# Eight units of an FFN input group in another order

## The chip, the core and the metric

One of the cores of a Trainium2 chip runs the whole program. The metric is the device time of one execution in microseconds (us); a difference is read from the medians of several executions of each kernel.

The core has five engines with queues of their own: TensorE (PE in the profile; PEld is its weight load), VectorE (DVE), ScalarE (ACT), GpSimd (POOL), and SyncE (SP), which here issues nearly all DMAs. Each works its instructions off in order. They meet only at semaphores: an instruction raises one when it is done, another waits until it has reached a value.

## What is computed

A block of 256 tokens by 2048 features passes a half-weighted gated FFN, a token mixer (mLSTM), a second such FFN, and a last norm. The change concerns the two FFNs alone, above all their first product:

```python
D_MODEL = 2048; SEQ = 256; D_FF = 5632
def swiglu_ffn(x, g, w_in, w_out):
    a, b = jnp.split(rmsnorm(x, g) @ w_in, 2, axis=-1)
    return (jax.nn.silu(a) * b) @ w_out
# h = h + 0.5 * swiglu_ffn(h, ffn_norm[i,0], ...)
# h = h + mlstm_mixer(rmsnorm(h), ...)
# h = h + 0.5 * swiglu_ffn(h, ffn_norm[i,1], ...)
# rmsnorm(h)
```

## The kernel before

**Split numbers.** All large products are made of float32 values split into a high and a low part. ACT copies raw weights into `w_hi` (rounded), DVE subtracts and writes `w_lo`, and PE makes three matmuls (high by high, low by high, high by low) for every product of a 128x128 activation block with a 128x512 weight block. The weights are streamed once: SP loads, ACT writes the high part, DVE the low part, PE uses both.

**Groups and units.** The 5632 hidden features of an FFN are made in 11 chunks of 512. The first chunk goes through a plain loop (line 534). The other ten are the *groups*: for each, `a` (left) and `b` (right) come from 16 blocks of 128 input rows. These 16 are taken in pairs, k and k+8, so a group has eight *units*, listed in `UNITS`. A unit that is *plain* makes 8 products (24 matmuls): the left half of its weights goes into the banks p2 and p4 (tokens 0 to 127 and 128 to 255), the right half into p5 and, with differences of activations, into p3. A unit that is *seven* makes a 2x2 block product with seven products (21 matmuls) from sums of activations (`s_hi`, `s_lo`) and mixed weights that DVE makes (`mix_weights`); it adds to p1, p2, p3, p5, p7, p6 and p4 in this order. Only the sevens write p1, p6 and p7. The order before is plain, seven, plain, seven, plain, seven, plain, plain.

**Items and slots.** A plain unit takes one *item* of split weights (two halves), a seven two items (straight weights, then mixed weights), so a group has 11 items. There are three slots for raw weights and three for split ones; ACT may write half of an item only when PE has used that half of the item three back (`pair_used`), and SP may load only when DVE is through with the raw unit three back (`pair_low`).

**Draining a group.** When a group's products are done they are gathered from the banks. ACT copies p1 (`keep_first`, line 1058). DVE then runs, in this order and in its one queue with the `w_lo` work: `drain_products` (p6 and p7 into `sums`; lines 1560, 1562; it waits for the last seven of the group), `drain_left` (p2 and p4 into `tile`; line 1569; it waits for the left half of unit 7), `drain_right` (p5; line 1576) and `drain_last` (p3; line 1583; it waits for all of unit 7). Each raises `drained`. PE may start the left half of the next group's first unit only after `drain_left`, its right half only after `drain_last`. ACT's `silu` and DVE's `gate_hidden` (line 1505) then make the hidden chunk, which PE turns (line 594, four 128x128 transposes each, after units 1 and 2 of the next group) and ACT keeps as `g32` (`keep_hidden`, line 1050).

**From the last group to the second product.** After group 9 the second product of the FFN starts (`ffn_out`; `plain` and `seven` units too, over `g_hi`, `g_lo`). Its first unit writes p2 and p4 again, and so waits for `drain_left` of group 9, as a next group would. DVE's queue at this place is: `w_lo` of units 6 and 7, `drain_products`, `low_hidden(0)` (line 1694), the two `w_lo` halves of the first output unit (line 1702), `low_hidden(1)`, `drain_left`, `drain_right`, `drain_last`. ACT's `high_hidden` (line 1115) writes `g_hi`, whose first two blocks lie over the buffer `mixed`.

Nothing is planned at run time: the order on every engine is the order in which the code is written.

Of the kernel before, what the change touches and what calls it, by code (L numbers as in the profile page):

```python
# [15 lines left out]
GK = 2  # L16
RING = 4
EPS = 1e-6
UNITS = (("plain", 3), ("seven", 0), ("plain", 4), ("seven", 1), ("plain", 5), ("seven", 2),
         ("plain", 6), ("plain", 7))  # L20
SEVENS, PLAINS = 3, 5
FIRST_ITEM = (0, 1, 3, 4, 6, 7, 9, 10)
ITEMS = 11
SLOTS = 3
DRAINS = 5
# [5 lines left out]
def trunk_program(nc, x, ffn_norm, ffn_w_in, ffn_w_out, mix_norm, a_w_in, a_b_if, a_head_norm,  # L31
# [38 lines left out]
    PAIR_HALVES = 2 * ITEMS * GROUPS  # L70
# [31 lines left out]
    def item(group, u):  # L102
        return ITEMS * group + FIRST_ITEM[u]

    def halves(i, n):
        return PAIR_HALVES * i + 2 * n
# [4 lines left out]
    with ExitStack() as ctx:  # L111
# [150 lines left out]
        pair_low = sem("pair_low")  # L262
        pair_used = sem("pair_used")
# [679 lines left out]
        def _(act):  # L943
# [83 lines left out]
            def high_straight(i, group, u):  # L1027

                n, unit = item(group, u), len(UNITS) * group + u
                act.wait_ge(left_landed[unit % SLOTS], landings(i, unit))  # L1030
                act.wait_ge(right_landed[unit % SLOTS], landings(i, unit))
                free(i, n, 1)
                nc.scalar.activation(hi_slots[n % SLOTS][:, 0:3], raw_slots[unit % SLOTS][:, 0:3], ACT.Copy)\  # L1033
                    .then_inc(pair_high, 2)
# [17 lines left out]

            def keep_first(i, group):

                act.wait_ge(pair_used, halves(i, item(group, 5)) + 1)
                if group:
                    act.wait_ge(drained, DRAINS * (GROUPS * i + group - 1) + 3)
                nc.scalar.activation(sums[:, 0, :], p1, ACT.Copy).then_inc(first_kept, 1)
# [11 lines left out]
            def ffn_in(i):  # L1070

                g = G_FFN[i]
                act.wait_ge(rstd_ready, 2 * i + 1)
                split(g + GD, 2, 3)
                silu_first(i)
                split(g + GD, 3, 5)
                high_sides(i)
                split(g + GD, 5, 6)
                high_differences(i)
                split(g + GD, 6, 8)  # L1080
                for group in range(GROUPS):
                    if group == 0:
                        high_plain(i, group, 0, 0)
                        high_plain(i, group, 0, 1)
                    high_straight(i, group, 1)
                    high_mixed(i, group, 1, 0)
                    if group:
                        silu(i, group - 1)
                    high_mixed(i, group, 1, 1)
                    high_plain(i, group, 2, 0)  # L1090
                    high_plain(i, group, 2, 1)
                    high_straight(i, group, 3)
                    keep_hidden(i, group, 0)
                    high_mixed(i, group, 3, 0)
                    high_mixed(i, group, 3, 1)
                    high_plain(i, group, 4, 0)
                    high_plain(i, group, 4, 1)
                    keep_hidden(i, group, 1)
                    high_straight(i, group, 5)
                    high_mixed(i, group, 5, 0)  # L1100
                    high_mixed(i, group, 5, 1)
                    high_plain(i, group, 6, 0)
                    high_plain(i, group, 6, 1)
                    keep_first(i, group)
                    high_plain(i, group, 7, 0)
                    high_plain(i, group, 7, 1)
                    if group < GROUPS - 1:
                        high_plain(i, group + 1, 0, 0)
                        high_plain(i, group + 1, 0, 1)

            def high_hidden(i, b):

                act.wait_ge(hidden_kept, 2 * (NF * i + b) + 2)
                act.wait_ge(pair_used, PAIR_HALVES * (i + 1) - (0 if b > 1 else 4))
                nc.scalar.activation(g_hi[:, 4 * b:4 * b + 4], g32[:, 4 * b:4 * b + 4], ACT.Copy)\
                    .then_inc(hidden_high, 1)

# [301 lines left out]
        def _(dve):  # L1419
# [116 lines left out]
            def mix_weights(i, group, u):  # L1536

                unit, s = len(UNITS) * group + u, SEVENS * (GROUPS * i + group) + UNITS[u][1]
                src = raw_slots[unit % SLOTS]
                if group == 0 and UNITS[u][1] == 0:  # L1540
                    dve.wait_ge(sides_low, 2 * i + 2)
                else:
                    pg, pu = (group, u - 2) if UNITS[u][1] else (group - 1, 5)
                    dve.wait_ge(pair_low, halves(i, item(pg, pu) + 2))
                dve.wait_ge(left_landed[unit % SLOTS], landings(i, unit))
                dve.wait_ge(right_landed[unit % SLOTS], landings(i, unit))
                nc.vector.tensor_tensor(mixed[:, 0:2], src[:, 0:3:2], src[:, 3:4].to_broadcast([P, 2, COLS]),
                                        ALU.subtract).then_inc(mixed_ready, 1)
                dve.wait_ge(mixed_ready, 3 * s + 1)
                nc.vector.tensor_tensor(mixed[:, 2], src[:, 2], mixed[:, 0], ALU.add).then_inc(mixed_ready, 1)  # L1550
                dve.wait_ge(mixed_ready, 3 * s + 2)
                nc.vector.tensor_tensor(mixed[:, 3], src[:, 1], mixed[:, 2], ALU.subtract)\
                    .then_inc(mixed_ready, 1)

            def drain_products(i, group):

                done = DRAINS * (GROUPS * i + group)
                dve.wait_ge(first_kept, GROUPS * i + group + 1)
                dve.wait_ge(pair_used, halves(i, item(group, 5) + 2))
                nc.vector.tensor_tensor(sums[:, 2], p6, sums[:, 0], ALU.add).then_inc(drained, 1)  # L1560
                dve.wait_ge(drained, done + 1)
                nc.vector.tensor_tensor(sums[:, 1], p7, sums[:, 2], ALU.add).then_inc(drained, 1)
# [76 lines left out]
            def ffn_in(i):  # L1639

                g = G_FFN[i]
                split(g + GD, 2, 3)
                sum_sides()
                split(g + GD, 3, 4)
                sum_differences()
                split(g + GD, 4, 5)
                low_sides(i)
                split(g + GD, 5, 6)
                low_differences(i)
                split(g + GD, 6, 8)  # L1650
                for group in range(GROUPS):
                    if group == 0:
                        low_plain(i, group, 0, 0)
                        low_plain(i, group, 0, 1)
                    mix_weights(i, group, 1)
                    low_straight(i, group, 1)
                    if group:
                        drain_left(i, group - 1)
                        low_mixed(i, group, 1, 0)
                        drain_right(i, group - 1)  # L1660
                        drain_last(i, group - 1)
                        low_mixed(i, group, 1, 1)
                        gate_hidden(i, group - 1)
                    else:
                        gate_first(i)
                        low_mixed(i, group, 1, 0)
                        low_mixed(i, group, 1, 1)
                    low_plain(i, group, 2, 0)
                    low_plain(i, group, 2, 1)
                    mix_weights(i, group, 3)  # L1670
                    low_straight(i, group, 3)
                    low_mixed(i, group, 3, 0)
                    low_mixed(i, group, 3, 1)
                    low_plain(i, group, 4, 0)
                    low_plain(i, group, 4, 1)
                    mix_weights(i, group, 5)
                    low_straight(i, group, 5)
                    low_mixed(i, group, 5, 0)
                    low_mixed(i, group, 5, 1)
                    low_plain(i, group, 6, 0)  # L1680
                    low_plain(i, group, 6, 1)
                    low_plain(i, group, 7, 0)
                    low_plain(i, group, 7, 1)
                    if group < GROUPS - 1:
                        low_plain(i, group + 1, 0, 0)
                        drain_products(i, group)
                        low_plain(i, group + 1, 0, 1)
                    else:
                        drain_products(i, group)

            def low_hidden(i, b):

# [446 lines left out]
```

## Time and profile before

| | us |
|---|---|
| Median of 3 executions (lowest, highest) | 1821.99 (1821.84, 1822.6) |
| The profiled execution, its own time | 1822.63 |
| Its span in the trace | 1820.9 |
| PE busy, share of the span | 1802.5, 99% |
| DVE busy | 1455.0, 80% |
| ACT busy | 976.5, 54% |
| Matmuls of lines 599 to 601 (all units, both FFNs) in the chain that ended last | about 70% |

The first number of a row of the timeline is the start in us from the start of the span, the second the time that the row's instructions took together, `x2` how many rows of one kind it merges; what stands in brackets is the idle time of that engine before it and who released it. A matmul's row says 0.39 us, but matmuls overlap: the pace of PE is the distance from one start to the next.

### The profile page before, as it was taken

To read this page: it belongs to the slowest core of one execution; us is meant where nothing else is said; L and a number is where in the kernel's file an instruction comes from. 1 tells how busy PE (TensorE), PEld (TensorE's weight loads), DVE (VectorE), ACT (ScalarE), POOL (GpSimd) and SP (SyncE) were. 2 spreads that over 40 slices of the span, in tenths; PEclk is the share of its full clock that TensorE was granted. 3 is DMA by queue.
4 is the path that set the end of the run, shared out by engine and by line. 5 is a ranking of instruction groups with operands and counts; after the bars stand their busy time and mean duration, and the time that the engine had idled before them with its cause. 6 is when DMAs were issued, how large, how long until landed. Compare 5 with 4: busy or idle time off the path is not lost.

```text
span 1820.9 us, 21509 instructions
## 1 busy us (share of the span) xinstructions
PE 1802.5 (99%) x8107; PEld 1488.4 (82%) x8107; DVE 1455.0 (80%) x1697; ACT 976.5 (54%) x1092; POOL 48.7 (3%) x58
## 2 busy tenths in 40 slices
PE   8999999999999999999999999999999999999998
PEld 6888888888888888888888888888888888888886
DVE  6888888888888886655478757888888888888787
ACT  6555555555555554544445445555555555555453
POOL 0000000000000002000000000000000000000002
PEclk9999999999999999999999999999999999999999
DMA  6666655556666556566645556666666556666564
GB/s 224 219 208 207 206 195 198 185 190 203 205 203 196 187 178 185 154 185 197 196 141 160 163 185 194 210 206 209 204 195 204 185 186 207 199 203 200 185 196 151
DMA packets 180612, 350.71 MB, mean 193 GB/s; under 512 B 10848, under 2 KB 11040, under 8 KB 180256
## 3 DMA queue, kind: packets, MB, share of 16 engines
q1 hardware_dynamic: 179952, 348.17, 59.5%
q0 software_dynamic: 432, 1.18, 0.2%
q8 instruction: 62, 1.02, 0.2%
q14 instruction: 38, 0.31, 0.1%
q10 hardware_dynamic: 128, 0.03, 0.0%
HBM read 347.24 MB, written 2.10 MB: 192 GB/s over the span
## 4 chain that ended last, share of the span: by engine, by line
PE 97%; ACT 1%; DVE 1%; issue 0%; DMA 0%; ACTq 0%; DVEq 0%
PE acc L534 23%; PE acc L599 12%; PE acc L601 12%; PE acc L600 12%; PE aux L599 11%; PE aux L601 11%; PE aux L600 11%; PE aux L594 1%; PE aux L563 1%; PE aux L902 1%; PE aux L890 0%; DMA h<-in_x_dram 0%; ACT u_hi L966 0%; PE aux L852 0%; DVE w_lo L1433 0%
## 5 line engine op out<-in xcount | busy, mean ns | idle before, releaser
L1433 DVE TENSOR_TENSOR w_lo<-raw,w_hi 128x1024 fp32r<-128x1024 f32 x160 | 194.9, 1229 | 107.7 <-ACT w_hi L951 106.2
L951 ACT ACTIVATE w_hi<-raw 128x1024 fp32r<-128x1024 f32 x160 | 168.4, 1059 | 123.6 <-PE acc L534 109.1
L534 PE MATMUL acc<-w_hi,u_hi 128*128 128x512 f32 x512 | 205.6, 401 | 4.2 <-DVE w_lo L1433 4.2
L534 PE MATMUL acc<-w_hi,u_lo 128*128 128x512 f32 x512 | 200.8, 392 | 0.0
L534 PE MATMUL acc<-w_lo,u_hi 128*128 128x512 f32 x512 | 200.3, 391 | 0.0
L1515 DVE TENSOR_TENSOR w_lo<-raw,w_hi 128x1024 fp32r<-128x1024 f32 x112 | 135.2, 1222 | 51.3 <-ACT w_hi L1024 51.3
L1024 ACT ACTIVATE w_hi<-raw 128x1024 fp32r<-128x1024 f32 x112 | 116.4, 1058 | 87.4 <-PE aux L601 46.4
L599 PE MATMUL acc<-w_hi,u_hi 128*128 128x512 f32 x358 | 140.7, 393 | 0.0
L601 PE MATMUL acc<-w_hi,u_lo 128*128 128x512 f32 x358 | 139.6, 390 | 0.0
L600 PE MATMUL acc<-w_lo,u_hi 128*128 128x512 f32 x358 | 139.4, 389 | 0.0
L534 PEld LDWEIGHTS acc<-w_hi,u_hi 128*128 128x128 f32 x512 | 96.7, 189 | 24.7 <-issue 5.0
L534 PEld LDWEIGHTS acc<-w_hi,u_lo 128*128 128x128 f32 x512 | 96.7, 189 | 21.0
L534 PEld LDWEIGHTS acc<-w_lo,u_hi 128*128 128x128 f32 x512 | 96.8, 189 | 19.2
L1702 DVE TENSOR_TENSOR w_lo<-raw,w_hi 128x1024 fp32r<-128x1024 f32 x62 | 75.0, 1233 | 27.6 <-ACT w_hi L1133 26.5
L1532 DVE TENSOR_TENSOR w_lo<-mixed,w_hi 128x1024 fp32r<-128x1024 f32 x72 | 85.7, 1218 | 1.7
L1133 ACT ACTIVATE w_hi<-raw 128x1024 fp32r<-128x1024 f32 x62 | 64.3, 1056 | 42.6 <-PE acc L601 19.8
L599 PE MATMUL acc<-w_hi,g_hi 128*128 128x512 f32 x216 | 84.4, 391 | 0.0
L1042 ACT ACTIVATE w_hi<-mixed 128x1024 fp32r<-128x1024 f32 x72 | 74.5, 1052 | 17.9 <-PE acc L601 17.9
L601 PE MATMUL acc<-w_hi,g_lo 128*128 128x512 f32 x216 | 84.1, 389 | 0.0
L600 PE MATMUL acc<-w_lo,g_hi 128*128 128x512 f32 x216 | 84.1, 389 | 0.0
L1033 ACT ACTIVATE w_hi<-raw 128x1536 fp32r<-128x1536 f32 x28 | 41.8, 1492 | 75.6 <-PE aux L601 66.8
L601 PE MATMUL aux<-w_hi,g_lo 128*128 128x512 f32 x205 | 79.8, 389 | 0.0
(322 smaller groups left out, 4523.6 us busy)
## 6 DMA issues: line engine op xcount, KB each, us to landing
raw<-in_ffn_w_in_dram SPq DMA_DIRECT2D x248, 512.0 KB, 4.5
raw<-in_ffn_w_out_dram SPq DMA_DIRECT2D x124, 512.0 KB, 4.9
raw_more<-in_ffn_w_in_dram SPq DMA_DIRECT2D x104, 512.0 KB, 4.5
raw<-in_a_w_in_dram SPq DMA_DIRECT2D x96, 512.0 KB, 4.2
raw_again<-in_ffn_w_out_dram SPq DMA_DIRECT2D x52, 512.0 KB, 5.4
raw<-in_a_w_out_dram SPq DMA_DIRECT2D x32, 512.0 KB, 4.4
h<-in_x_dram SPq DMA_DIRECT2D x4, 512.0 KB, 8.8
final_gain<-in_final_norm_dram POOLq DMA_DIRECT2D x1, 1024.0 KB, 6.8
```

The lines of the kernel that those rows point to most:

```text
L534: mm = nc.tensor.matmul(acc[:, TT * (c % 2) + t, :], s[:, k, tok], w[:, ring, kk, :], start=(k == 0 and n == 0), stop=(k == GK * granules ...
L599: nc.tensor.matmul(bank, side_hi, wide_hi, start=start, stop=False)
L600: nc.tensor.matmul(bank, side_hi, wide_lo, start=False, stop=False)
L601: return nc.tensor.matmul(bank, side_lo, wide_hi, start=False, stop=stop)
L951: nc.scalar.activation(w_hi[:, n % RING], raw[:, n % RING], ACT.Copy)\
L1024: nc.scalar.activation(hi_slots[n % SLOTS][:, at], raw_slots[unit % SLOTS][:, at], ACT.Copy)\
L1042: nc.scalar.activation(hi_slots[n % SLOTS][:, at], mixed[:, at], ACT.Copy)\
L1133: nc.scalar.activation(out_hi[n % SLOTS][:, at], out_raw[slot][:, at], ACT.Copy)\
L1433: nc.vector.tensor_tensor(w_lo[:, n % RING], raw[:, n % RING], w_hi[:, n % RING].bitcast(F32), ALU.subtract)\
L1515: nc.vector.tensor_tensor(lo_slots[n % SLOTS][:, at], raw_slots[unit % SLOTS][:, at], hi_slots[n % SLOTS][:, at].bitcast(F32), ALU.subtract)\
L1532: nc.vector.tensor_tensor(lo_slots[n % SLOTS][:, at], mixed[:, at], hi_slots[n % SLOTS][:, at].bitcast(F32), ALU.subtract)\
L1702: nc.vector.tensor_tensor(out_lo[n % SLOTS][:, at], out_raw[slot][:, at], out_hi[n % SLOTS][:, at].bitcast(F32), ALU.subtract)\
```

## The change

`UNITS` and the item numbers get another order: plain, plain, seven, plain, seven, plain, seven, plain. A group's last seven is now unit 6 of 7 (before, unit 5 of 7), and its first is unit 2. The bodies of the loops on ACT and DVE are written in the new order; `keep_first` and `drain_products` wait for the last seven at its new place; `drain_left`, `drain_right` and `drain_last` stand among the `w_lo` work of unit 1 of the next group. In `ffn_out` nothing is written anew but the wait of the first two `high_hidden`, which is now for the `w_lo` of the last seven (the last reader of `mixed`).

```diff
-UNITS = (("plain", 3), ("seven", 0), ("plain", 4), ("seven", 1), ("plain", 5), ("seven", 2),
-         ("plain", 6), ("plain", 7))
+UNITS = (("plain", 3), ("plain", 4), ("seven", 0), ("plain", 5), ("seven", 1), ("plain", 6),
+         ("seven", 2), ("plain", 7))
-FIRST_ITEM = (0, 1, 3, 4, 6, 7, 9, 10)
+FIRST_ITEM = (0, 1, 2, 4, 5, 7, 8, 10)
@@ keep_first (ACT)
-                act.wait_ge(pair_used, halves(i, item(group, 5)) + 1)
+                act.wait_ge(pair_used, halves(i, item(group, 6)) + 1)
@@ high_hidden (ACT)
-                act.wait_ge(pair_used, PAIR_HALVES * (i + 1) - (0 if b > 1 else 4))
+                if b > 1:
+                    act.wait_ge(pair_used, PAIR_HALVES * (i + 1))
+                else:
+                    act.wait_ge(pair_low, PAIR_HALVES * (i + 1) - 2)
@@ drain_products (DVE)
-                dve.wait_ge(pair_used, halves(i, item(group, 5) + 2))
+                dve.wait_ge(pair_used, halves(i, item(group, 6) + 2))
@@ ffn_in (DVE)
-                    mix_weights(i, group, 1)
-                    low_straight(i, group, 1)
+                    low_plain(i, group, 1, 0)
                     if group:
                         drain_left(i, group - 1)
-                        low_mixed(i, group, 1, 0)
+                        low_plain(i, group, 1, 1)
                         drain_right(i, group - 1)
                         drain_last(i, group - 1)
-                        low_mixed(i, group, 1, 1)
+                        mix_weights(i, group, 2)
                         gate_hidden(i, group - 1)
...
                     if group < GROUPS - 1:
                         low_plain(i, group + 1, 0, 0)
-                        drain_products(i, group)
                         low_plain(i, group + 1, 0, 1)
-                    else:
-                        drain_products(i, group)
+                    drain_products(i, group)
```

The first place is DVE's queue from one group to the next. `w_lo` rows of 128x1024 are half a plain unit, the 128x1536 row is the straight part of a seven, `mixed` rows are its mixed weights; `sums<-acc,sums` are `drain_products`, `tile<-acc,sums` is `drain_left`, `sums<-aux,sums` of 128x1024 and 128x512 are `drain_right` and `drain_last`. Before:

```order
L1515 TENSOR_TENSOR w_lo<-raw,w_hi 128x1024 [waits pair_high] x3
L1560 TENSOR_TENSOR sums<-acc,sums 128x512 [waits pair_used,first_kept]
L1562 TENSOR_TENSOR sums<-acc,sums 128x512 [waits drained]
L1515 TENSOR_TENSOR w_lo<-raw,w_hi 128x1024 [waits pair_high]
L1547 TENSOR_TENSOR mixed<-raw_more 128x1024 [waits right_landed2,left_landed2,pair_low]
L1550 TENSOR_TENSOR mixed<-raw_more,mixed 128x512 [waits mixed_ready]
L1552 TENSOR_TENSOR mixed<-raw_more,mixed 128x512 [waits mixed_ready]
L1523 TENSOR_TENSOR w_lo_more<-raw_more,w_hi_more 128x1536 [waits pair_high]
L1569 TENSOR_TENSOR tile<-acc,sums 128x1024 [waits drained,hidden_turned,pair_used]
L1532 TENSOR_TENSOR w_lo<-mixed,w_hi 128x1024 [waits pair_high]
L1576 TENSOR_TENSOR sums<-aux,sums 128x1024 [waits drained,right_summed]
L1583 TENSOR_TENSOR sums<-aux,sums 128x512 [waits drained,pair_used]
```

The same place after (line numbers are three higher there):

```order
L1518 TENSOR_TENSOR w_lo<-raw,w_hi 128x1024 [waits pair_high] x4
L1563 TENSOR_TENSOR sums<-acc,sums 128x512 [waits pair_used,first_kept]
L1565 TENSOR_TENSOR sums<-acc,sums 128x512 [waits drained]
L1518 TENSOR_TENSOR w_lo_more<-raw_more,w_hi_more 128x1024 [waits pair_high]
L1572 TENSOR_TENSOR tile<-acc,sums 128x1024 [waits drained,hidden_turned,pair_used]
L1518 TENSOR_TENSOR w_lo_more<-raw_more,w_hi_more 128x1024 [waits pair_high]
L1579 TENSOR_TENSOR sums<-aux,sums 128x1024 [waits drained,right_summed]
L1586 TENSOR_TENSOR sums<-aux,sums 128x512 [waits drained,pair_used]
```

Between `drain_products` and `drain_left` there stood five instructions and there now stands one; the mixing of weights has moved behind `drain_last`.

The second place is DVE's queue at the end of the last group, where the second product of the FFN begins (`g_lo` is `low_hidden`; the `w_lo` row between the two is the first output unit). Before:

```order
L1523 TENSOR_TENSOR w_lo<-raw_more,w_hi 128x1536 [waits pair_high]
L1532 TENSOR_TENSOR w_lo_more<-mixed,w_hi_more 128x1024 [waits pair_high] x2
L1515 TENSOR_TENSOR w_lo<-raw,w_hi 128x1024 [waits pair_high] x4
L1560 TENSOR_TENSOR sums<-acc,sums 128x512 [waits pair_used,first_kept]
L1562 TENSOR_TENSOR sums<-acc,sums 128x512 [waits drained]
L1694 TENSOR_TENSOR g_lo<-g,g_hi 128x1024 [waits hidden_high]
L1702 TENSOR_TENSOR w_lo<-raw,w_hi 128x1024 [waits out_high] x2
L1694 TENSOR_TENSOR g_lo<-g,g_hi 128x1024 [waits hidden_high]
L1569 TENSOR_TENSOR tile<-acc,sums 128x1024 [waits drained,hidden_turned,pair_used]
```

After:

```order
L1526 TENSOR_TENSOR w_lo_more<-raw,w_hi_more 128x1536 [waits pair_high]
L1535 TENSOR_TENSOR w_lo<-mixed,w_hi 128x1024 [waits pair_high] x2
L1518 TENSOR_TENSOR w_lo<-raw,w_hi 128x1024 [waits pair_high] x2
L1563 TENSOR_TENSOR sums<-acc,sums 128x512 [waits pair_used,first_kept]
L1565 TENSOR_TENSOR sums<-acc,sums 128x512 [waits drained]
L1695 TENSOR_TENSOR g_lo<-g,g_hi 128x1024 [waits hidden_high]
L1703 TENSOR_TENSOR w_lo<-raw,w_hi 128x1024 [waits out_high] x2
L1695 TENSOR_TENSOR g_lo<-g,g_hi 128x1024 [waits hidden_high]
L1572 TENSOR_TENSOR tile<-acc,sums 128x1024 [waits drained,hidden_turned,pair_used]
```

The seven now ends one plain unit later: four halves of `w_lo` stood between it and the drain, two stand there now. From `drain_products` on the order is the same.

## Rows read from the trace of the kernel before

**Rows 1.** Waits of PE: what waited for what, total us, times, longest.
```profile
PE acc L534 <- DVE w_lo L1433: 4.2, 4, 2.4
```
**Rows 2.** Timeline of PE, first turn of two groups in succession.
```profile
282.23 0.60 PE L594 MATMUL aux<-ident,tile 128*128 128x128 f32 x4
...
324.68 0.60 PE L594 MATMUL aux<-ident,tile 128*128 128x128 f32 x4
```
**Rows 3.** Timeline of PE, last group: start of unit 7, start of the output.
```profile
478.82 0.39 PE L599 MATMUL acc<-w_hi,u_hi 128*128 128x512 f32 x1
...
484.26 0.39 PE L599 MATMUL acc<-w_hi,g_hi 128*128 128x512 f32 x1
```
**Rows 4.** Timeline of DVE, end of the last group.
```profile
471.76 2.36 DVE L1515 TENSOR_TENSOR w_lo<-raw,w_hi 128x1024 fp32r<-128x1024 f32 x2 [0.56 <-ACT w_hi L1024]
474.04 0.68 DVE L1560 TENSOR_TENSOR sums<-acc,sums 128x512 f32<-128x512 f32 x1
...
475.36 1.22 DVE L1694 TENSOR_TENSOR g_lo<-g,g_hi 128x1024 fp32r<-128x1024 f32 x1
...
481.31 1.22 DVE L1694 TENSOR_TENSOR g_lo<-g,g_hi 128x1024 fp32r<-128x1024 f32 x1
482.45 1.22 DVE L1569 TENSOR_TENSOR tile<-acc,sums 128x1024 f32<-128x1024 f32 x1
```
**Rows 5.** Timeline of PE, a matmul of the mixer that starts as another chunk ends.
```profile
1040.55 0.39 PE L534 MATMUL acc<-w_hi,y_hi 128*128 128x512 f32 x1
```
**Rows 6.** Timeline of DVE, the instruction that the end of that chunk releases.
```profile
1040.74 1.29 DVE L1634 SCALAR_TENSOR_TENSOR tile<-acc,h 128x512 f32<-128x512 f32 x2 [0.34 <-PE acc L534]
```
**Rows 7.** Timeline of DVE, a drain in the second FFN's output.
```profile
1694.71 1.22 DVE L1804 SCALAR_TENSOR_TENSOR tile<-acc,tile 128x1024 f32<-128x1024 f32 x1
```
**Rows 8.** Timeline of PE, which waits for that drain.
```profile
1695.38 0.39 PE L601 MATMUL aux<-w_hi,g_lo 128*128 128x512 f32 x1
1695.98 0.50 PE L599 MATMUL acc<-u_hi,g_hi 128*128 128x512 f32 x1 [0.22 <-DVE tile L1804]
1696.32 0.40 PE L600 MATMUL acc<-u_lo,g_hi 128*128 128x512 f32 x1
```
**Rows 9.** Timeline of ACT, end of the last group.
```profile
470.18 0.60 ACT L1058 ACTIVATE sums<-aux 128x512 f32<-128x512 f32 x1 [0.24 <-PE acc L601]
...
476.36 1.06 ACT L1133 ACTIVATE w_hi<-raw 128x1024 fp32r<-128x1024 f32 x1 [1.66 <-PE acc L601]
```
**Rows 10.** Timeline of PE, second FFN: start of the output.
```profile
1577.68 0.39 PE L599 MATMUL acc<-w_hi,g_hi 128*128 128x512 f32 x1
```
**Rows 11.** Timeline of DVE, second FFN: drain_left of the last group.
```profile
1575.87 1.22 DVE L1569 TENSOR_TENSOR tile<-acc,sums 128x1024 f32<-128x1024 f32 x1
```
**Rows 12.** Timeline of PE, group boundary: right half of unit 7, next group.
```profile
269.31 0.39 PE L599 MATMUL aux<-w_hi,u_hi 128*128 128x512 f32 x1
...
272.03 0.39 PE L599 MATMUL acc<-w_hi,u_hi 128*128 128x512 f32 x1
```
**Rows 13.** Timeline of DVE at that boundary: the drains.
```profile
270.14 1.22 DVE L1569 TENSOR_TENSOR tile<-acc,sums 128x1024 f32<-128x1024 f32 x1
...
272.40 1.22 DVE L1576 TENSOR_TENSOR sums<-aux,sums 128x1024 f32<-128x1024 f32 x1
273.72 0.69 DVE L1583 TENSOR_TENSOR sums<-aux,sums 128x512 f32<-128x512 f32 x1
```
**Rows 14.** The page's DMA issues: count, size, median us from issue to landing.
```profile
raw<-in_ffn_w_in_dram SPq DMA_DIRECT2D x248, 512.0 KB, 4.5
```
**Rows 15.** Timeline of PE, start of the mixer: the longest wait of PE in mid-program.
```profile
739.39 0.39 PE L534 MATMUL acc<-w_hi,u_lo 128*128 128x512 f32 x1
740.69 0.47 PE L534 MATMUL acc<-w_hi,u_hi 128*128 128x512 f32 x1 [0.91 <-DVE w_lo L1433]
```
**Rows 16.** Timeline of PE, two of the twelve matmuls from 9.84 us on.
```profile
14.24 0.63 PE L534 MATMUL acc<-w_lo,u_hi 128*128 128x512 f32 x1
14.67 0.63 PE L534 MATMUL acc<-w_hi,u_lo 128*128 128x512 f32 x1
```

More of the change, by code:

```diff
@@ L1084, in ffn_in @@
                         high_plain(i, group, 0, 1)
-                    high_straight(i, group, 1)
-                    high_mixed(i, group, 1, 0)
+                    high_plain(i, group, 1, 0)
+                    high_plain(i, group, 1, 1)
                     if group:
                         silu(i, group - 1)
[L1089 to L1092, printed above, removed]
+                    high_straight(i, group, 2)
+                    high_mixed(i, group, 2, 0)
+                    high_mixed(i, group, 2, 1)
+                    high_plain(i, group, 3, 0)
+                    high_plain(i, group, 3, 1)
                     keep_hidden(i, group, 0)
[L1094 to L1097, printed above, removed]
+                    high_straight(i, group, 4)
                     keep_hidden(i, group, 1)
[L1099 to L1104, printed above, removed]
+                    high_mixed(i, group, 4, 0)
+                    high_mixed(i, group, 4, 1)
+                    high_plain(i, group, 5, 0)
+                    high_plain(i, group, 5, 1)
+                    high_straight(i, group, 6)
+                    high_mixed(i, group, 6, 0)
+                    high_mixed(i, group, 6, 1)
                     high_plain(i, group, 7, 0)
                     high_plain(i, group, 7, 1)
+                    keep_first(i, group)
                     if group < GROUPS - 1:
@@ L1542, in mix_weights @@
                 else:
-                    pg, pu = (group, u - 2) if UNITS[u][1] else (group - 1, 5)
+                    pg, pu = (group, u - 2) if UNITS[u][1] else (group - 1, 6)
                     dve.wait_ge(pair_low, halves(i, item(pg, pu) + 2))
@@ L1665, in ffn_in @@
                         gate_first(i)
[L1666 to L1681, printed above, removed]
+                        low_plain(i, group, 1, 1)
+                        mix_weights(i, group, 2)
+                    low_straight(i, group, 2)
+                    low_mixed(i, group, 2, 0)
+                    low_mixed(i, group, 2, 1)
+                    low_plain(i, group, 3, 0)
+                    low_plain(i, group, 3, 1)
+                    mix_weights(i, group, 4)
+                    low_straight(i, group, 4)
+                    low_mixed(i, group, 4, 0)
+                    low_mixed(i, group, 4, 1)
+                    low_plain(i, group, 5, 0)
+                    low_plain(i, group, 5, 1)
+                    mix_weights(i, group, 6)
+                    low_straight(i, group, 6)
+                    low_mixed(i, group, 6, 0)
+                    low_mixed(i, group, 6, 1)
                     low_plain(i, group, 7, 0)
```

## The prediction, made before the changed kernel ran

> **What bounds the kernel now.** I read the waits of PE first, then the timeline of PE across several groups, then DVE and ACT at the places where PE depends on them.
>
> PE is the bound without a gap. Its waits on other engines in the whole span, apart from the load of the input, are 4.2 us for `w_lo` in the plain loops [rows 1] and 0.22 us for one drain in an output stage [rows 8]; none lies in the twenty groups. The groups come at a fixed period: the same turn is at 282.23 and at 324.68, so 42.45 us [rows 2], which is 183 matmuls (5 x 24 + 3 x 21) and eight short transposes. A plain unit takes 484.26 - 478.82 = 5.44 us for 24 matmuls [rows 3], 0.2267 us each; a seven, 21 of them, takes 4.76 us. The change leaves every matmul, DMA and split in place. So in the groups it can gain nothing: where PE never waits there is no wait to remove. What can change is that PE meets a wait which was hidden, and the question is how much room each of them has.
>
> Two waits have little room. I call B the moment at which PE is through with unit 7 and wants to start the next stretch.
>
> At a boundary between groups B = 272.03 [rows 12]. `drain_left` ended at 270.14 + 1.22 = 271.36, `drain_last` at 273.72 + 0.69 = 274.41 [rows 13]. PE wants the first at B and the second at B + 2.72 = 274.75 (half a plain unit later): room of 0.67 and 0.34 us.
>
> At the end of the last group B = 484.26 [rows 3]; `drain_left` ended at 482.45 + 1.22 = 483.67 [rows 4]: room of 0.59 us. The second FFN repeats this: 1575.87 + 1.22 = 1577.09 against 1577.68 [rows 10, 11].
>
> **The change at a boundary between groups (18 times).** The last seven now ends at B - 5.44, not at B - 10.88. `drain_products` needs it. How fast DVE answers to PE: a matmul's successor starts at 1040.55, the DVE instruction that this end released at 1040.74 [rows 5, 6], so 0.19 us. ACT answers in 0.26: its row at 476.36 was released by the left half that ended at 484.26 - 5.44 - 2.72 = 476.10 [rows 3, 9].
>
> ACT comes first. `keep_first` needs the first two products of the seven, at B - 10.20 + 1.36 = B - 8.84; it starts at B - 8.58 and takes 0.60 [rows 9]. Then two ACT copies of at most 1.06 each [rows 9] for the next group's unit 0 end by B - 5.9, and DVE's second half of `w_lo` for it by about B - 4.7 (1.22 each [rows 4]). `drain_products` could start at B - 5.44 + 0.19 = B - 5.25 and starts at B - 4.7. It takes 475.36 - 474.04 = 1.32 [rows 4]: B - 3.4. One half `w_lo` follows; back to back such an instruction costs 482.45 - 481.31 = 1.14 [rows 4] (the pair of 2.36 at 471.76 is the same, 1.14 + 1.22): B - 2.26. `drain_left` may start from B - 2.72 + 0.19, so it starts at B - 2.26 and ends at B - 1.04. A second half `w_lo` ends its turn at B + 0.02, `drain_right` passes in 273.72 - 272.40 = 1.32 [rows 13], and `drain_last` ends at B + 1.34 + 0.69 = B + 2.03, wanted at B + 2.72. Room 1.04 and 0.69 us, more than before. Cost: nothing. The mixing for the seven, now behind `drain_last`, is wanted at B + 10.88, and is done by about B + 7.5 (three instructions, `gate_hidden`, the straight part): room of over 3 us. Loads wait for `w_lo` of the unit three back, whose DVE work ends at least 7 us before B for all three first units, against 4.5 us from issue to landing [rows 14]. What hides all this is PE's own work; the cover is 1.04 and 0.69 us, and each 0.1 us by which a drain overran it would cost 18 x 0.1 = 1.8 us.
>
> **The change at the end of the last group (twice).** Here DVE's queue has more between `drain_products` and `drain_left`: `low_hidden(0)`, two halves of the first output unit, `low_hidden(1)`. Before, the first of them started long before PE needed the drain (`drain_products` at B - 10.22 [rows 3, 4]), and DVE idled between them. Now the queue stops at `drain_products` until B - 5.25. DVE is free from B - 7.6: ACT's copy of unit 7's right half is released at B - 10.20 + 0.26, and 1.06 + 1.22 later `w_lo` is through; `keep_first` is done at B - 8.0 as above. So the start is set by PE's seven, and the rest is a sum:
>
> start B - 5.44 + 0.19 = B - 5.25; `drain_products` 1.32; four instructions of 128x1024 back to back at 1.14 = 4.56; `drain_left` 1.22. End: B + 1.85.
>
> Does ACT hold it up? Its copies for the first output unit need the two halves of the seven's second item, used at B - 6.80 and B - 5.44, so they end at latest at B - 5.5 and B - 3.5, `high_hidden(1)` between them at B - 4.5, each before DVE comes to it (B - 2.8 to B - 0.5). The new condition on `high_hidden` (`w_lo` of the last seven, about B - 11.4) is met long before. No.
>
> PE restarts after the drain. Where it waits for one before, the drain ends at 1694.71 + 1.22 = 1695.93 and PE starts at 1695.98 [rows 7, 8]: 0.05; the next matmul comes 0.34 later and not 0.23 [rows 8], 0.11 more. So one transition costs 1.85 + 0.05 + 0.11 = 2.01 us, two cost 4.0 us. Bounds for one: none at all if the drain came in its 0.59 us of room as before; 2.7 if each of the five back-to-back instructions before the drain took the 0.1 more that single ones show to PE's restart elsewhere (740.69 comes 1.30 after 739.39, and a copy before it may be late by as much [rows 15]). I take the sum, since all its terms are rows of the same instructions in the same place.
>
> What is late next: `drain_last` then ends at B + 1.85 + 0.10 + 1.32 + 0.69 = about B + 4.0, wanted at B + 1.90 + 2.72 = B + 4.6; `w_lo` of the second output unit by B + 6.6, its left half by B + 5.5, wanted from B + 7.4. These hold, with 0.6 us as the least.
>
> Sum against the profiled execution: 1822.63 + 4.0 = 1826.6; its own time is 0.64 above the median of the runs, so the median goes from 1821.99 to 1826.0. A measurement of this kernel tells about 0.2% from no change, 3.6 us; the forecast is just beyond it.
>
> **Rivals.**
>
> 1. The delay is taken back later. In the first FFN's wake PE waits in the mixer's start (1.30 us from 739.39 to 740.69, of which 0.23 is its pace [rows 15]), and it waits 0.6 - 0.23 = 0.37 before 1695.98 [rows 8]; all `w_lo` waits together are 4.2 us, the longest 2.4 of them at the start [rows 1]. If these hung on DMA or on work that doesn't move with PE, up to 4.2 - 2.4 = 1.8 and 0.4 us would be absorbed: 4.0 - 2.2 = 1.8 us, 1823.8, not slower by what can be told. For it: those are waits on DVE and ACT, not on PE. Against it: their chains begin with results that PE has just made. It decides if PE's waits after the stall shrink.
>
> 2. The groups stall too. The boundary keeps 0.69 us of room by a sum of many terms. If DVE's queue there is a microsecond later than I make it, `drain_last` costs some 0.3 us each time: 18 x 0.3 + 4.0 = 9.4, 1831.4. For it: before, the room was as small, so nothing is loose. Against: the sum gives more room than before with the same instructions.
>
> 3. The clock falls in the new gap. Before, twelve matmuls after the first wait came 14.67 - 14.24 = 0.43 us apart [rows 16], 512 columns at 1.2 GHz, against 0.227 at 2.4 GHz later. Twelve such after each gap of 1.9 us cost 2 x 12 x 0.20 = 4.8 more: 1830.8. Against: after the 0.91 us idle before 740.69 the engine went on with 0.47 us for a matmul, not 0.63 [rows 15]. No row has a gap of 1.9 us at full clock. The Trainium skill (TensorE: Matmul & The Clock Gate, section HAM oscillation) warns of just this, waits between bursts of matmuls that bring the clock down each time; no run here shows how long a gap must be.
>
> 4. The order does nothing: no wait of PE appears, 1822.0. It would need the last seven's products to be free earlier than B - 5.44; the order of DVE's rows speaks against it.
>
> **How the numbers follow.** Forecast 0.70, of which 0.12 for a sum that comes out under 3.6 us (it is 4.0, with some 0.2 for the answer times and as much for the medians). Rival 1: 0.11. Rival 2: 0.07. Rival 3: 0.05. Rival 4 and what I overlook, 0.07: half of it no change, half divided between faster (0.03) and slower. So slower 0.58 + 0.07 + 0.05 + 0.01 = 0.71, same 0.12 + 0.11 + 0.03 = 0.26, faster 0.03. The range of the forecast alone is 1825.2 to 1827.4 (2.7 a time at the top). To hold eight in ten it reaches down to rival 1 and up a little beyond the forecast's bound: 1823.6 to 1828.4.
>
> **What would show it.** In the changed kernel's waits of PE a row appears for the output's matmul (line 599) on `tile` of `drain_left` (line 1572), twice, some 1.7 us each. The period of the groups stays at 42.45. DVE idles before line 1563 in the last group and starts it 5.25 us before PE would be through; `drain_left` follows 5.88 later. At group boundaries `drain_left` ends about 1.0 us before PE's next group. Wrong would be: any wait of PE within the groups, matmuls 0.43 apart after the gap, or the waits at the mixer's start gone.

## The result, and the profile after

The changed kernel takes 1826.62 us in the median of 11 executions (1825.69 to 1828.94) against 1822.05 (1821.73 to 1822.88) before: 4.57 us slower. The ratio over all executions is 1.0029 with the interval 1.0021 to 1.0037, which excludes 1, no change; that of the medians alone is 1.0025. The forecast was 1826.0. The executions fall in two bunches: six of 1825.69 to 1826.62 and five of 1828.59 to 1828.94. The median is the last of the lower bunch; the profiled execution, 1828.94 us with a span of 1827.2, belongs to the upper one.

The waits of PE in the changed kernel (what waited for what: total us, times, longest), with one row more than before [rows 1]:

```profile
PE acc L534 <- DVE w_lo L1436: 4.2, 4, 2.4
PE acc L798 <- DMA first_rows<-in_ffn_norm_dram: 3.9, 1, 3.9
PE acc L599 <- DVE tile L1572: 3.6, 2, 1.8
PE aux L563 <- DMA h<-in_x_dram: 1.4, 1, 1.4
PE acc L599 <- DVE tile L1805: 0.2, 1, 0.2
```

The third row is new: twice, PE waits 1.8 us for `drain_left`. The others stand as before within 0.2 us. The timeline of DVE at the end of the last group, to be read against [rows 4]:

```profile
475.83 1.23 DVE L1518 TENSOR_TENSOR w_lo<-raw,w_hi 128x1024 fp32r<-128x1024 f32 x1 [1.31 <-ACT w_hi L1024]
479.51 0.69 DVE L1563 TENSOR_TENSOR sums<-acc,sums 128x512 f32<-128x512 f32 x1 [2.45 <-PE acc L601]
480.24 0.69 DVE L1565 TENSOR_TENSOR sums<-acc,sums 128x512 f32<-128x512 f32 x1
480.85 1.21 DVE L1695 TENSOR_TENSOR g_lo<-g,g_hi 128x1024 fp32r<-128x1024 f32 x1
481.98 2.35 DVE L1703 TENSOR_TENSOR w_lo<-raw,w_hi 128x1024 fp32r<-128x1024 f32 x2
484.25 1.22 DVE L1695 TENSOR_TENSOR g_lo<-g,g_hi 128x1024 fp32r<-128x1024 f32 x1
485.39 1.22 DVE L1572 TENSOR_TENSOR tile<-acc,sums 128x1024 f32<-128x1024 f32 x1
```

Before `drain_products` (line 1563) DVE is idle for 2.45 us; then seven instructions follow one another without a pause, `drain_left` (line 1572) as the last. It ends at 486.61. The timeline of PE there:

```profile
484.46 0.39 PE L601 MATMUL aux<-w_hi,d_lo 128*128 128x512 f32 x1
486.65 0.50 PE L599 MATMUL acc<-w_hi,g_hi 128*128 128x512 f32 x1 [1.81 <-DVE tile L1572]
487.00 0.54 PE L600 MATMUL acc<-w_lo,g_hi 128*128 128x512 f32 x1
487.33 0.63 PE L601 MATMUL acc<-w_hi,g_lo 128*128 128x512 f32 x1
487.76 0.63 PE L599 MATMUL acc<-w_hi,g_hi 128*128 128x512 f32 x1
...
490.32 0.49 PE L599 MATMUL acc<-w_hi,g_hi 128*128 128x512 f32 x1
```

From 484.46 to 486.65 there are 2.19 us in place of 0.23: the gap costs 1.96. And behind it the matmuls come 0.43 us apart, with 0.63 as their length, as at the program's start [rows 16]. The table of stretches (PE, PEld, DVE, ACT, POOL busy; granted clock; DMA) shows the clock with it:

```profile
480.00:486.00 6.00, 4.84 (x22) 3.68 (x20) 5.97 (x7) 1.10 (x2) 0.00 (x0) 1.00 0.15 51
486.00:490.00 4.00, 3.35 (x9) 2.63 (x10) 3.57 (x4) 3.37 (x5) 0.00 (x0) 0.64 0.94 296
```

The clock granted had been 1.00 (2.4 GHz) and has a mean of 0.64 in the next stretch: for a part of it the lower level, 1.2 GHz. At the second FFN the gap is the same, the fall is missing:

```profile
1581.58 0.39 PE L601 MATMUL aux<-w_hi,d_lo 128*128 128x512 f32 x1
1583.78 0.50 PE L599 MATMUL acc<-w_hi,g_hi 128*128 128x512 f32 x1 [1.81 <-DVE tile L1572]
1584.11 0.39 PE L600 MATMUL acc<-w_lo,g_hi 128*128 128x512 f32 x1
```

A boundary between groups, DVE, to be read against [rows 13]:

```profile
270.12 1.22 DVE L1572 TENSOR_TENSOR tile<-acc,sums 128x1024 f32<-128x1024 f32 x1
...
273.71 0.69 DVE L1586 TENSOR_TENSOR sums<-aux,sums 128x512 f32<-128x512 f32 x1
```

and PE, first matmul of the next group:

```profile
272.45 0.39 PE L599 MATMUL acc<-w_hi,u_hi 128*128 128x512 f32 x1
```

So B = 272.45; `drain_left` ends at 271.34 and `drain_last` at 274.40, rooms of 1.11 and 0.77 us (before 0.67 and 0.34). The period is unchanged; the first turns of two groups:

```profile
240.89 0.60 PE L594 MATMUL aux<-ident,tile 128*128 128x128 f32 x4
...
283.34 0.60 PE L594 MATMUL aux<-ident,tile 128*128 128x128 f32 x4
```

42.45 us as in [rows 2].

### The profile page after: what moved, and what is told of

Same layout as the page of the kernel before. It is cut to its first block, busy times and chain, and to the rows that moved or that the text cites. A ratio compares the mean times of both kernels' runs of the same rounds, so it can differ in the third digit from the quotient of the medians.

```text
span 1827.2 us, 21509 instructions
## 1 busy us (share of the span) xinstructions
PE 1805.0 (99%) x8107; PEld 1489.8 (82%) x8107; DVE 1452.3 (79%) x1697; ACT 979.3 (54%) x1092; POOL 48.9 (3%) x58
## 4 chain that ended last, share of the span: by engine, by line
PE 97%; DVE 1%; ACT 1%; issue 1%; DMA 0%; ACTq 0%; DVEq 0%
PE acc L534 23%; PE acc L599 12%; PE acc L601 12%; PE acc L600 12%; PE aux L601 11%; PE aux L599 11%; PE aux L600 11%; PE aux L594 1%; PE aux L563 1%; PE aux L902 1%; PE aux L890 0%; DVE w_lo L1703 0%; DMA h<-in_x_dram 0%; ACT u_hi L966 0%; PE aux L852 0%
## 5 line engine op out<-in xcount | busy, mean ns | idle before, releaser
L1042 ACT ACTIVATE w_hi<-mixed 128x1024 fp32r<-128x1024 f32 x84 | 87.4, 1058 | 43.0 <-PE aux L601 19.7
L1535 DVE TENSOR_TENSOR w_lo<-mixed,w_hi 128x1024 fp32r<-128x1024 f32 x84 | 98.9, 1219 | 8.7 <-ACT w_hi L1042 8.7
L599 PE MATMUL aux<-w_hi,g_hi 128*128 128x512 f32 x205 | 79.7, 389 | 0.0
```

Source lines behind the costliest of these rows:

```text
L599: nc.tensor.matmul(bank, side_hi, wide_hi, start=start, stop=False)
L1042: nc.scalar.activation(hi_slots[n % SLOTS][:, at], mixed[:, at], ACT.Copy)\
L1535: nc.vector.tensor_tensor(lo_slots[n % SLOTS][:, at], mixed[:, at], hi_slots[n % SLOTS][:, at].bitcast(F32), ALU.subtract)\
```

## The experiments

Theory after this reading: the cost in every execution is the drain of the last group, which comes too late twice, 4.1 us; the rest is a clock that falls behind the gap in part of the executions. Rivals: some of it comes from the groups, or from the new order on ACT and SP.

| kernel | median us | lowest to highest | executions | kernel before beside it | ratio, interval |
|---|---|---|---|---|---|
| e0_again | 1827.55 | 1826.22 to 1828.88 | 6 | 1822.31 | 1.0030, 1.0018 to 1.0042 |
| e1_drain_early | 1822.67 | 1821.96 to 1823.59 | 11 | 1822.31 | 1.0003, 0.9994 to 1.0012 |
| e2_before_late_drain | 1826.57 | 1826.04 to 1828.91 | 9 | 1822.31 | 1.0028, 1.0018 to 1.0038 |
| e3_one_behind | 1824.38 | 1823.64 to 1825.12 | 11 | 1822.31 | 1.0011, 1.0002 to 1.0020 |
| e4_first_only | 1824.32 | 1823.92 to 1826.92 | 11 | 1822.41 | 1.0016, 1.0007 to 1.0025 |
| e5_second_only | 1825.32 | 1824.80 to 1826.13 | 11 | 1822.41 | 1.0016, 1.0007 to 1.0025 |
| e6_one_more | 1830.44 | 1830.32 to 1830.79 | 4 | 1822.41 | 1.0043, 1.0027 to 1.0058 |
| e7_two_more | 1834.59 | 1834.09 to 1835.68 | 4 | 1822.41 | 1.0067, 1.0052 to 1.0083 |
| e8_second_again (kernel of e5_second_only) | 1825.72 | | 1 | 1822.12 | |
| e9_second_third (the same) | 1825.78 | | 1 | 1822.12 | |
| e10_two_moves | 1822.15 | 1821.74 to 1822.71 | 11 | 1822.26 | 1.0000, 0.9991 to 1.0009 |

**The change once more (e0_again).** No edit.

> The changed kernel once more, for its spread and a second profile. Theory (two late drains, and a clock that falls after a gap in some executions): two gaps of 1.96 us before the first output matmul of each FFN in every execution, 4.1 us in all over the kernel before; executions in which the matmuls after a gap run at half pace lie 2.6 us higher, so times come in two bunches, near 1826.1 and 1828.7. Rival (the rest above 4.1 us is noise of starting up): one bunch.

Three executions at 1826.22 to 1826.42, three at 1828.68 to 1828.88: two bunches. The profiled one (1826.42, span 1824.7) has both gaps and no slow matmul behind them. Its timeline of PE at the first gap and at the second:

```profile
485.66 0.50 PE L599 MATMUL acc<-w_hi,g_hi 128*128 128x512 f32 x1 [1.81 <-DVE tile L1572]
486.00 0.40 PE L600 MATMUL acc<-w_lo,g_hi 128*128 128x512 f32 x1
...
1581.23 0.50 PE L599 MATMUL acc<-w_hi,g_hi 128*128 128x512 f32 x1 [1.81 <-DVE tile L1572]
```

From the restart to the next gap's end it has 1581.23 - 485.66 = 1095.57 us; the first profile has 1583.78 - 486.65 = 1097.13. The fall costs 1.56 us. The remaining 0.99 us between these two executions lies ahead of the gap (486.65 against 485.66), in the program's start. Twelve matmuls of line 534 stand there, then eight transposes (line 563), then line 534 again. In the first profile all twelve are slow, and line 534 goes on at 16.40:

```profile
14.75 0.63 PE L534 MATMUL acc<-w_hi,u_lo 128*128 128x512 f32 x1
15.18 1.47 PE L563 MATMUL aux<-ident,h 128*128 128x128 f32 x8
16.40 0.47 PE L534 MATMUL acc<-w_hi,u_hi 128*128 128x512 f32 x1
```

Here full pace begins at the tenth of the twelve, and line 534 goes on at 15.39:

```profile
13.90 0.39 PE L534 MATMUL acc<-w_hi,u_hi 128*128 128x512 f32 x1
14.13 0.40 PE L534 MATMUL acc<-w_lo,u_hi 128*128 128x512 f32 x1
...
15.39 0.47 PE L534 MATMUL acc<-w_hi,u_hi 128*128 128x512 f32 x1
```

I call the start of this first matmul behind the transposes the *mark*: the earlier full pace begins, the earlier it comes. 1.56 + 0.99 = 2.55, the spans differ by 2.5. The lower bunch lies 3.9 to 4.1 us over the kernel before. One execution of an upper bunch was profiled in all, and three of lower bunches (here, e2_before_late_drain, e4_first_only); the other executions are put down to one or the other by their times alone.

**The drain moved ahead (e1_drain_early).**

```diff
                 low_hidden(i, 0)
                 out_low_plain(i, 0, 0)
-                out_low_plain(i, 0, 1)
-                low_hidden(i, 1)
                 drain_left(i, GROUPS - 1)
+                out_low_plain(i, 0, 1)
                 drain_right(i, GROUPS - 1)
                 drain_last(i, GROUPS - 1)
+                low_hidden(i, 1)
```

> The changed kernel, with drain_left of the last group moved ahead in VectorE's queue: behind low_hidden(0) and the first half of the first output unit, and low_hidden(1) moved behind drain_last. Theory (the order in the groups costs nothing, all of it is the drain chain at the end of the last group): no gap, the time of the kernel before, 1822.0 +- 0.4. Rival (the groups or the start-up cost something too): 1823 or more.

1822.67, 0.36 us over the kernel before beside it (1822.31, itself above the 1822.0 of the expectation); the interval of the ratio, 0.9994 to 1.0012, takes in 1, no change. The row `tile L1572` is gone from PE's waits. With it go the groups as a suspect for the 4.1 us: this kernel has them all in the new order. A small rest is left at the right half of the first output unit; PE:

```profile
486.20 0.39 PE L601 MATMUL acc<-w_hi,g_lo 128*128 128x512 f32 x1
486.48 0.50 PE L599 MATMUL aux<-w_hi,g_hi 128*128 128x512 f32 x1
486.82 0.40 PE L600 MATMUL aux<-w_lo,g_hi 128*128 128x512 f32 x1
```

and DVE:

```profile
485.73 0.69 DVE L1586 TENSOR_TENSOR sums<-aux,sums 128x512 f32<-128x512 f32 x1
```

`drain_last` ends at 486.42, 0.28 and then 0.34 us stand for 0.23: 0.16 us a time.

**The late wait alone, in the kernel before (e2_before_late_drain).**

```diff
-                dve.wait_ge(pair_used, halves(i, item(group, 5) + 2))
+                dve.wait_ge(pair_used, halves(i, item(group, 6 if group == GROUPS - 1 else 5) + (1 if group == GROUPS - 1 else 2)))
```

> The kernel before, with one number changed: in the last group alone drain_products waits until unit 6 is used (one plain unit later), as it must in the new order. Theory: both gaps of 1.96 us appear though no unit has moved, +4.1 us, and +2.6 more in executions in which the clock falls; 1826.1 or 1828.7. Rival (the gap comes from ScalarE's or SyncE's new order at the end): no change, 1822.0.

1826.57, six executions at 1826.04 to 1826.70 and three at 1828.79 to 1828.91: both bunches of the change, in a kernel whose units, loads and ACT queue are those of before. Its waits of PE hold the same row:

```profile
PE acc L599 <- DVE tile L1569: 3.6, 2, 1.8
```

The moment at which DVE may pass `drain_products` in the last group is enough for all of the cost, and the rival, the new order on ACT and SP, falls.

**A shorter gap (e3_one_behind).** Only `low_hidden(1)` moved:

```diff
                 out_low_plain(i, 0, 1)
-                low_hidden(i, 1)
                 drain_left(i, GROUPS - 1)
                 drain_right(i, GROUPS - 1)
                 drain_last(i, GROUPS - 1)
+                low_hidden(i, 1)
```

> The changed kernel, with low_hidden(1) alone moved behind drain_last of the last group. Theory: drain_left comes one back-to-back instruction (1.14 us) earlier, the gap is 1.96 - 1.14 = 0.82, with 0.1 for the restart 0.9 a time: +1.8 us, 1823.9. If it is the length of the gap that lets the clock fall, no execution shows it; if any gap does, some are 2 to 3 us higher.

1824.38, 2.07 over the kernel before, one bunch. PE's gap:

```profile
484.46 0.39 PE L601 MATMUL aux<-w_hi,d_lo 128*128 128x512 f32 x1
485.53 0.50 PE L599 MATMUL acc<-w_hi,g_hi 128*128 128x512 f32 x1 [0.68 <-DVE tile L1572]
485.87 0.40 PE L600 MATMUL acc<-w_lo,g_hi 128*128 128x512 f32 x1
```

1.07 - 0.23 = 0.84, and 0.11 for the restart: 0.95 a time. One instruction of 1.14 us out of the chain shortens the gap by 1.12. Nothing shows a fall: the profiled execution has no slow matmul behind either gap, and the lowest and the highest execution lie 2.2 and 2.0 us over the lowest and the highest of the kernel before, about what two such gaps make. The mark of the profiled one is 16.37, as late as in the profile with the fall (16.40): with as late a start, the clock stood behind a gap of less than half the length.

**One gap only (e4_first_only, e5_second_only).** The order of e1_drain_early in the other FFN:

```diff
-                out_low_plain(i, 0, 1)
-                low_hidden(i, 1)
-                drain_left(i, GROUPS - 1)
+                if i == 0:        # e5_second_only: i == 1
+                    out_low_plain(i, 0, 1)
+                    low_hidden(i, 1)
+                    drain_left(i, GROUPS - 1)
+                else:
+                    drain_left(i, GROUPS - 1)
+                    out_low_plain(i, 0, 1)
                 drain_right(i, GROUPS - 1)
                 drain_last(i, GROUPS - 1)
+                if not (i == 0):  # e5_second_only: i == 1
+                    low_hidden(i, 1)
```

> The changed kernel with the early drain of e1_drain_early in the second FFN only: one gap, in the first FFN. Theory: half of the cost, 2.05 us a gap, 1824.4; in part of the executions the clock falls at this gap (the profile of the changed kernel had it here), and they lie about 2.5 us higher. Rival (the two gaps hang together): anything but half.

Six executions at 1823.92 to 1824.32 and five at 1826.65 to 1826.92. The lower bunch is about the half that was expected, 1.5 to 1.9 us over 1822.41 in place of 2.05 (the profiled one, 1823.93, has the earliest mark of all, 14.92); the upper stands 2.8 higher, median against median. This gap alone makes both bunches.

> The changed kernel with the early drain in the first FFN only: one gap, in the second FFN. Theory: 1824.4 again. If each gap can let the clock fall on its own, there is an upper bunch here too; no execution of the full change has shown both falls (4.1 + 2 x 1.6 us and more), so if only the first gap can, all executions lie near 1824.4.

1825.32, one bunch from 1824.80 to 1826.13, 2.9 us over the kernel before and not 2.05. The expectation had no room for that, and the profile of this run (1824.88 us) has no slow matmul behind the gap. So the same kernel was profiled twice more.

> The kernel of e5_second_only for a second profile. Its eleven executions lay 2.9 us above the kernel before, where one gap without a fall of the clock makes 2.05. Theory: in part of the executions some matmuls behind the second gap are slow, which the first profile, of 1824.88, didn't have; a profile of 1825.5 or more shows 4 or 5 matmuls 0.43 us apart after 1579. Rival: the rest lies in the start of the program, and the matmuls behind the gap keep 0.23.

> The same kernel once more, for a third profile; the same two theories.

1825.72 and 1825.78 us, and both have the fall. PE in e8_second_again:

```profile
1579.03 0.50 PE L599 MATMUL acc<-w_hi,g_hi 128*128 128x512 f32 x1 [1.81 <-DVE tile L1572]
...
1580.29 0.58 PE L601 MATMUL acc<-w_hi,g_lo 128*128 128x512 f32 x1
1580.67 0.63 PE L599 MATMUL acc<-w_hi,g_hi 128*128 128x512 f32 x1
1581.09 0.63 PE L600 MATMUL acc<-w_lo,g_hi 128*128 128x512 f32 x1
```

The engine goes on at full pace for five matmuls (three in e9_second_third) and only then slows, so the fall isn't the restart's own cost. It made about eight slow matmuls, not the four or five expected. From the restart to the end of the span it is 1824.0 - 1579.03 = 244.97 us, and without a fall (e5_second_only, restart at 1579.76) 1823.2 - 1579.76 = 243.44: 1.5 us, about the price of the fall at the first gap.

The mark is at 15.22 and 15.17 us in these two, at 15.93 in the one without a fall. So here early starters fell: they had won 0.7 us at the start and lost 1.5 at the gap, 0.8 us in all. At the first gap it is the late starter (16.40) that fell, and the two losses add up to 2.55. That would explain why one bunch shows here and two there, but three profiles don't show it, and how many of the eleven executions fell isn't known.

**Longer gaps (e6_one_more, e7_two_more).** One or two more subtractions ahead of the drain:

```diff
                 out_low_plain(i, 0, 0)
+                dve.wait_ge(out_high, out_half(i, 0) + 2)
+                for _ in range(1):        # e7_two_more: 2
+                    link(nc.vector.tensor_tensor(out_lo[0][:, 2:4], out_raw[0][:, 2:4],
+                                                 out_hi[0][:, 2:4].bitcast(F32), ALU.subtract))
                 out_low_plain(i, 0, 1)
```

> The changed kernel with one w_lo subtraction of the first output unit made twice, ahead of the drain (the result is the same). Theory: each gap is longer by that instruction, 1.22 + 0.1 for its own wait: 3.2 us, and 6.6 us in all with the restarts: 1828.9 where the clock holds. If longer gaps let it fall more often, most executions show one fall or two, 1.6 us and more each: 1830.5 to 1833.

1830.44, 8.0 over the kernel before, just under the 1830.5 to 1833 that were expected with falls; four executions within 0.5 us. The profile has gaps of 3.24 us, slow matmuls behind the first and none behind the second: 2 x (3.24 + 0.11) + 1.56 = 8.3. Its mark is early, 15.33; at 1.96 us none of the three profiles with so early a mark fell at the first gap.

> The same subtraction made three times: gaps of 4.5 us, 9.2 us in all: 1831.5 where the clock holds. If the length decides, the clock falls at both gaps in every execution and the time is 1835 to 1837; the matmuls behind each gap stand 0.43 us apart.

1834.59, 12.2 over the kernel before, a little under the range given; gaps of 4.49 us, slow matmuls behind both in the profiled execution. PE in e7_two_more:

```profile
483.26 0.39 PE L601 MATMUL aux<-w_hi,d_lo 128*128 128x512 f32 x1
487.98 0.80 PE L599 MATMUL acc<-w_hi,g_hi 128*128 128x512 f32 x1 [4.33 <-DVE tile L1572]
488.58 0.63 PE L600 MATMUL acc<-w_lo,g_hi 128*128 128x512 f32 x1
```

Here the very first matmul is slow already.

**Two moves (e10_two_moves).** As e1_drain_early, and `low_hidden(0)` in DVE's idle time:

```diff
                         low_plain(i, group + 1, 0, 1)
+                    else:
+                        low_hidden(i, 0)
                     drain_products(i, group)
@@ ffn_out (DVE)
-                low_hidden(i, 0)
                 out_low_plain(i, 0, 0)
```

> The changed kernel with two moves in VectorE's queue at the end of the last group: low_hidden(0) ahead of drain_products, where the engine idled for 2.45 us, and drain_left ahead of the second half of the first output unit, with low_hidden(1) behind drain_last. Theory: e1_drain_early still had drain_last 0.05 us late, which with the restart costs 0.16 us a time; here the drains come 1.14 us earlier and nothing is late: all of the cost of the change is gone, 1822.2, and 0.3 us less than e1_drain_early. Rival (something of the new order in the groups remains): as e1_drain_early.

1822.15 against 1822.26, ratio 1.0000 (0.9991 to 1.0009). PE's waits are those of the kernel before, and DVE has room again:

```profile
476.47 1.23 DVE L1697 TENSOR_TENSOR g_lo<-g,g_hi 128x1024 fp32r<-128x1024 f32 x1 [0.56 <-ACT g_hi L1118]
478.36 0.69 DVE L1563 TENSOR_TENSOR sums<-acc,sums 128x512 f32<-128x512 f32 x1 [0.67 <-PE acc L601]
...
481.01 1.23 DVE L1572 TENSOR_TENSOR tile<-acc,sums 128x1024 f32<-128x1024 f32 x1
...
484.60 0.69 DVE L1586 TENSOR_TENSOR sums<-aux,sums 128x512 f32<-128x512 f32 x1
```

`drain_left` ends at 482.24 and PE wants it at 483.53; `drain_last` ends at 485.29 and is wanted at 486.25. The new order of the units, with its end put right, costs nothing that can be told from no change, and brings nothing. No version here beats the kernel before, and none could by this way: PE had no wait in the groups to give back.

## Why the prediction was right, point by point

- **PE has nothing to gain in the groups**: right. Period 42.45 us before and after; with the end mended (e10_two_moves) the time is that of before.
- **The groups keep their cover**: right. Rooms of 1.04 and 0.69 us were worked out, 1.11 and 0.77 are there. Rival 2 falls.
- **The drain of the last group comes late, twice**: right, and shown both ways: e10_two_moves takes the cost away, e2_before_late_drain makes it alone.
- **The size, 2.01 us a time**: the medians of the lower bunches are 4.1 over the kernel before (the changed kernel, e0_again, e2_before_late_drain). The chain from `drain_products` to `drain_left` was put at 5.88 and is 485.39 - 479.51 = 5.88. Only the answer of DVE to PE was short: the start was put 0.19 us after the last seven's end and came at 479.51 - (484.46 + 0.23 - 5.44) = 0.26. So the gap is 1.96 and not 1.90, with the restart 2.07. The upper bound of 2.7 doesn't follow from its terms: 2.01 + 5 x 0.1 is 2.5, with the late copy 2.6.
- **Rival 1, given back later**: wrong. PE's wait at the mixer's start is still 1.30 from start to start (743.52 to 744.82), the `w_lo` waits are 4.2 in all, the drain of line 1805 0.2 [rows 1, 8, 15].
- **Rival 3, the clock**: this is what the forecast underrated. It was given 0.05, for a fall at both gaps, 2.4 us each. The upper bunch holds 5 of 11 executions, and the one of them that was profiled has the fall at one gap, for 1.56 us. The prediction itself named matmuls 0.43 us apart after the gap as a sign of being wrong, and they are there. The argument against it, that the engine went on at full pace after 0.91 us of idle time [rows 15], was right for a gap of that length (e3_one_behind agrees) and says nothing on one twice as long. That the median came out 0.6 us from the forecast is luck: six of eleven executions lie in the lower bunch, and all five of the upper one (1828.59 and more) lie above the range of 1823.6 to 1828.4. With one more of them the median would have too. The mean of the eleven, 1827.3, is 5.1 over that of the kernel before, and the ratio of 1.0029 is near that of the means. The Trainium skill warns of waits between bursts of matmuls that bring the clock down each time (TensorE: Matmul & The Clock Gate, section HAM oscillation). The trace agrees in kind, with a granted clock of 0.64 behind one of the gaps, but not in "each time": behind the other gap of the same length the clock stood.

What stays open: why some executions fall and others don't. The length of the gap has a part in it: with a late mark (16.37, 16.40) the clock stood behind 0.84 us and fell behind 1.96, and with an early mark it stood at the first gap behind 1.96 us (14.92 to 15.39, three profiles) and fell behind 3.24 (15.33). At the same length, 1.96 us, the fall at the first gap goes with a late mark, and at the second gap alone with an early one (15.22, 15.17; 15.93 without it). These are few profiles, and no run varied the start on purpose.

## What to carry to other kernels

When units are reordered under an engine that never waits, look not at the units but at the last of each loop: the drain that waits for the moved unit has a queue behind it, and the last pass has another queue than the others. Add up that queue from the release to the instruction that the busy engine wants, and move whatever isn't wanted yet (here one block of `g_lo`, half of `w_lo`) behind it or into the idle time ahead of it. A gap of some 2 us in a stream of matmuls can have a price beyond its length, here in part of the executions: look at the single executions, not at the median alone.

## What the runs showed of the hardware that was not expected

Behind gaps that cost 0.84 us (e3_one_behind, 11 executions, one bunch) no fall of the clock showed; behind one of 1.96 us in the first FFN 5 of 11 executions lie in the upper bunch (e4_first_only), behind two of them 11 of 26 (the changed kernel, e0_again, e2_before_late_drain); behind one of 1.96 us in the second FFN two of three profiles have a fall, though the times form one bunch; with 3.24 us the four executions lie together and the profile has one fall; with 4.49 us it has two. A fall makes some eight matmuls 0.43 us apart and costs about 1.56 us. It can begin five matmuls after the engine has restarted at full pace.
